# Expert results put to their tokens by TensorE job by job instead of through memory, a third short expert job, and the last weight unit in two transfers

## The reference, cut to what matters

```python
def _moe(xn, router, w_gu, w_down):
    logits = (xn @ router).astype(jnp.float32)
    top_v, top_i = lax.top_k(logits, TOP_K)          # 2 of 8 experts
    w = jax.nn.softmax(top_v, axis=-1)
    gates = jnp.sum(w[..., None] * jax.nn.one_hot(top_i, N_EXPERTS, dtype=jnp.float32), axis=-2)
    y = jnp.zeros_like(xn)
    for e in range(N_EXPERTS):
        y = y + gates[..., e:e + 1].astype(xn.dtype) * _swiglu(xn, w_gu[e], w_down[e])
    return y
...
x = x + _moe(_rmsnorm(x, norm_g[l, 1]), ...)
return _rmsnorm(x, final_norm_g)
```

## Time and profile before

| | before |
|---|---|
| median of 3 runs | 1277.41 us (1275.36 to 1279.4) |
| the profiled execution: device time | 1277.48 us |
| the profiled execution: span | 1275.7 us |
| TensorE busy | 1243.6 us (97%) |
| VectorE, ScalarE busy | 398.6 us (31%), 270.5 us (21%) |
| mean granted TensorE clock | 0.997 |
| bytes moved | 437.87 MB, mean 343 GB/s |

### The profile page before, as it was taken

How to read it: one execution, slowest core, us unless ns; L and a number is a source line. 1 busy time by engine, 2 the same in 40 slices (tenths; PEclk the granted TensorE clock), 3 DMA queues, 4 the chain that set the end, 5 groups by cost and what they waited for, 6 DMA issues and landing times.

```text
span 1275.7 us, 24518 instructions
## 1 busy us (share of the span) xinstructions
PE 1243.6 (97%) x11007; PEld 645.1 (51%) x11007; DVE 398.6 (31%) x665; ACT 270.5 (21%) x396; POOL 31.0 (2%) x71
## 2 busy tenths in 40 slices
PE   8999999999999999999989999999999999999975
PEld 7988888888888633333423333333333333333321
DVE  6886665677675502002002100300200030020022
ACT  6765455455464200000000000000000000000001
POOL 2000000002000100000000000000000000000010
PEclk9999999999999999999999999999999999999999
DMA  9654655556916899999999999999999999999995
GB/s 347 201 184 153 211 180 181 197 187 212 321 57 255 341 415 376 422 427 431 429 429 428 430 429 428 430 428 424 428 390 419 411 367 427 401 427 410 428 429 240
DMA packets 84836, 437.87 MB, mean 343 GB/s; under 512 B 4728, under 2 KB 47840, under 8 KB 61184
## 3 DMA queue, kind: packets, MB, share of 16 engines
q1 hardware_dynamic: 80896, 423.64, 82.3%
q0 software_dynamic: 2912, 10.06, 2.5%
q10 hardware_dynamic: 928, 2.68, 0.5%
HBM read 425.87 MB, written 10.49 MB: 342 GB/s over the span
## 4 chain that ended last, share of the span: by engine, by line
PE 91%; DMA 7%; DVE 1%; ACT 1%; issue 0%; ACTq 0%; DVEq 0%; POOLq 0%; SPq 0%; POOL 0%
PE bank L1915 40%; PE bank L1937 12%; PE bank L1565 8%; PE bank L1531 6%; PE bank L1944 6%; PE bank L1532 5%; PE bank L1533 5%; DMA ring<-in_moe_w_gu 4%; PE bank L1564 3%; DMA ring<-in_moe_w_down 3%; PE bank L1972 1%; PE bank L1645 1%; PE bank L1568 0%; PE bank L1822 0%; PE bank L1796 0%; PE bank L1768 0%
## 5 line engine op out<-in xcount | busy, mean ns | idle before, releaser
L1915 PE MATMUL bank<-ring,tokT 128*32 128x512 f32 (+1 forms) x5632 | 533.1, 539 | 2.5 <-DMA ring<-in_moe_w_gu 1.5
L1915 PEld LDWEIGHTS bank<-ring,tokT 128*32 128x32 f32 x5632 | 184.7, 110 | 348.0 <-issue 336.1
L1937 PE MATMUL bank<-ring,hT 128*32 128x512 f32 x1568 | 176.9, 592 | 3.9 <-DMA ring<-in_moe_w_down 3.9
L879 DVE TENSOR_TENSOR w_lo<-raw,w_hi 128x2048 fp32r<-128x2048 f32 x62 | 141.8, 2290 | 50.4 <-ACT w_hi L515 50.1
L1565 PE MATMUL bank<-act_parts,w_hi 128*128 128x512 f32 x368 | 127.5, 396 | 0.0
L1396 DVE TENSOR_TENSOR y_sb<-bank,yc_part 32x512 f32<-32x512 f32 x12 | 8.2, 684 | 377.4 <-ACT yc_part L810 377.3
L515 ACT ACTIVATE w_hi<-raw 128x2048 fp32r<-128x2048 f32 x62 | 118.4, 1913 | 28.1 <-PE bank L1533 28.1
L793 ACT ACTIVATE silu_e<-bank 128x1024 f32<-128x1024 f32 x8 | 8.2, 1024 | 493.4 <-PE bank L1915 493.4
L1937 PEld LDWEIGHTS bank<-ring,hT 128*32 128x32 f32 x1568 | 51.2, 110 | 120.3 <-issue 112.7
L1564 PE MATMUL bank<-act_parts,w_lo 128*128 128x256 f32 x322 | 89.8, 279 | 0.0
L1944 PE MATMUL bank<-ring,hT 128*32 128x512 f32 x672 | 79.8, 592 | 0.0
(11 more groups left out here) (331 smaller groups left out, 1080.3 us busy)
## 6 DMA issues: line engine op xcount, KB each, us to landing
ring<-in_moe_w_gu SPq DMA_DIRECT2D x128, 1792.0 KB, 15.2
ring<-in_moe_w_down SPq DMA_DIRECT2D x56, 2048.0 KB, 17.3
raw<-in_mlp_w_gu SPq DMA_DIRECT2D x22, 1024.0 KB, 4.9
raw<-in_mlp_w_down SPq DMA_DIRECT2D x11, 1024.0 KB, 4.8
raw<-in_lru_w_in SPq DMA_DIRECT2D x8, 1024.0 KB, 11.0
raw<-in_w_kvf SPq DMA_DIRECT2D x8, 1024.0 KB, 5.1
raw<-in_fox_w_qg SPq DMA_DIRECT2D x8, 1024.0 KB, 5.3
y_rows<-zeros POOLq DMA_DIRECT2D x17, 384.0 KB, 12.4
```

Source lines behind the costliest of these rows:

```text
L879: v.tensor_tensor(split_of(u)[1][:, :], raw[:, u % RAW, :], split_of(u)[0][:, :].bitcast(f32), ALU.subtract).then_inc(lo_done, 1)
L1915: last = t_.matmul(b[32 * t:32 * t + 32, 0:N1 if s else N0], tokT[:, g, k, :], of_tile[:, t, 4:7, :] if s else of_tile[:, t, 0:4, :], star ...
L1937: last = t_.matmul(y_ab_ps[32 * t:32 * t + 32, :], hidden_of(u, r, t % 2), w[:, lo:lo + HALF], start=u == 0 and r == 0, stop=u == 6 and r ...
```

## The change

Results of jobs 0 to 6 no longer go through `y_rows`. A table `place` is built once: for each of a token's two choices it holds, on every partition, the token's row number and its weight (`place_by_column`: eight diagonal matrices by VectorE, two matmuls with ones, one copy). For each job VectorE compares the row numbers with the slot numbers `slot_n` of the job and gets `w_T`, the weight of each token in each slot (`weights_by_slot`). TensorE multiplies `w_T` with `y_sb` (`place_y`, once for each 128 tokens, two matmuls of 128 x 512 each), into banks 6 and 7, and VectorE adds them to `x` (`add_y`). Third, `BY_COUNT` and `SHORT_OF` make job `middle + 3` (the fifth, job 4 where there are 8 jobs) short too. Last, the last down unit comes in two transfers of 1024 KB with a wait for each (`last_unit`), and the load of the final gain waits for the first matmuls of that unit.

```diff
-BY_COUNT = (0, 1, 3, 4, 5, 6, 7, 2)
+BY_COUNT = (0, 1, 4, 5, 3, 6, 7, 2)
...
-            for u in range(7):
+            for u in range(6):
                 sp.wait_ge(unit_used, used_in(last, u - 6))
                 down(last, last_expert, u)
+            sp.wait_ge(unit_used, used_in(last, 0))
+            for rr in range(2):
+                of = slice(2 * D * rr, 2 * D * rr + 2 * D)
+                sp.dma_start(deep_slot(6)[:, of], e_dn[last_expert][:, 6, of]).then_inc(slot_full[6 + rr], 16)
...
-            for j in range(NE - 1, ROUNDS * NE):
-                pool.dma_start(y_rows[CAP * j:CAP * j + CAP, :], zeros[0:CAP, :]).then_inc(y_blank, 16)
...
             pool.wait_ge(xsg_ready, NT)
+            pool.wait_ge(y_half, 1)
             pool.dma_start(gain_bc[:], final_norm_g.partition_broadcast(P)).then_inc(gfin_loaded, 16)
...
-            for t in range(NT):
-                for c, into in enumerate((xs, xs_g)):
-                    g.indirect_dma_start(out=into[:, t, :], out_offset=None, in_=y_rows[:, :],
-                                         in_offset=bass.IndirectOffsetOnAxis(ap=row_i[:, c, t:t + 1], axis=0)).then_inc(y_back[t][c], 16)
...
-                act.dma_start(y_rows[bass.ds(CAP * j, n), :], y_sb[0:n, :]).then_inc(y_stored, 16)
...
-                v.tensor_scalar(of_count(SHORT_OF), of_count(PLACE), float(2), None, ALU.is_le)
+                v.tensor_scalar(of_count(SHORT_OF), of_count(PLACE), float(3), None, ALU.is_le)
...
+            def add_y(j):
+                for t in range(NT):
+                    dve.wait_ge(y_placed, 2 * j + t + 1)
+                    v.tensor_tensor(x[:, t, :], banks2[3][:], x[:, t, :], ALU.add).then_inc(y_added, 1)
...
+                for n, of_token in enumerate((row_f[:, 0, :, :], gate_t[:])):
+                    for c in range(2):
+                        for t in range(NT):
+                            last = v.tensor_scalar(of_rows(n)[:, c, t, :], ident[:], of_token[:, c, t:t + 1], None, ALU.mult)
+                last.then_inc(diag_built, 1)
+                dve.wait_ge(place_done, 1)
+                v.tensor_copy(place[:].rearrange("p n c m -> p (n c m)"), banks2[3][:]).then_inc(place_ready, 1)
...
+                for c in range(2):
+                    last = v.scalar_tensor_tensor(out=w_T[0:CAP, c, :], in0=place[0:CAP, 0, c, :], scalar=slot_n[0:CAP, 0:1], in1=place[0:CAP, 1, c, :],
+                                                  op0=ALU.is_equal, op1=ALU.mult)
...
-            for n in range(4):
-                t, c = n // 2, n % 2
-                dve.wait_ge(y_back[t][c], 16)
-                v.scalar_tensor_tensor(out=x[:, t, :], in0=(xs, xs_g)[c][:, t, :], scalar=gate_t[:, c, t:t + 1], in1=x[:, t, :],
-                                       op0=ALU.mult, op1=ALU.add).then_inc(moe_added, 1)
...
+            def place_y(j, t, short=False):
+
+                n = SHORT if short else CAP
+                for half in range(2):
+                    last = t_.matmul(bank[6 + half], w_T[0:n, 0, t * P:(t + 1) * P], y_sb[0:n, HALF * half:HALF * half + HALF],
+                                     start=True, stop=True)
+                last.then_inc(y_placed, 1)
...
                 for k in range(KD):
-                    if more and k == 4:
+                    if k == 1:
                         pe.wait_ge(y_free_a, j + 1)
-                        pe.wait_ge(y_free_d, sums_now)
+                        pe.wait_ge(y_free_d, sums)
+                        pe.wait_ge(w_built, 2 * j + 2)
+                        place_y(j, 0, short)
+                    if k == 3:
+                        pe.wait_ge(y_added, 2 * j + 1)
+                        place_y(j, 1, short)
+                    if more and k == 5:
+                        pe.wait_ge(y_added, 2 * j + 2)
                         gather_tokens(j + 2)
```

More of the change, by code:

```diff
@@ L801, in expert_silu, with copy_y @@
                     a.activation(silu_e[:, C0:WIDTH], c_ps, ACT.Silu).then_inc(e_silu, 1)
-            def copy_y(j, stored=None, short=False):
+            def copy_y(j, short=False):
                 act.wait_ge(unit_used, used_in(j, 15))
-                if stored is not None:
-                    act.wait_ge(y_stored, stored)
                 for half in range(2):
@@ L1946, in down, with last_rounds @@
                 last.then_inc(unit_used, 1)
+            def last_rounds(w, u, half, rr):
+                for t in range(4):
+                    r = 2 * rr + t // 2
+                    lo = r * D + half * HALF
+                    last = t_.matmul(y_half_ps[half][32 * t:32 * t + 32, :], hidden_of(u, r, t % 2), w[:, lo:lo + HALF],
+                                     start=u == 0 and rr == 0, stop=u == 6 and rr == 1)
+                return last
             def last_down(fill, u):
@@ L1954, in last_down, with last_unit @@
                     for rr in range(2):
-                        for t in range(4):
-                            r = 2 * rr + t // 2
-                            lo = r * D + half * HALF
-                            last = t_.matmul(y_half_ps[half][32 * t:32 * t + 32, :], hidden_of(u, r, t % 2), w[:, lo:lo + HALF],
-                                             start=u == 0 and rr == 0, stop=u == 6 and rr == 1)
-                    if half == 1:
-                        last.then_inc(unit_used, 1)
-                    elif u == 6:
-                        last.then_inc(y_half, 1)
+                        last = last_rounds(w, u, half, rr)
+                last.then_inc(unit_used, 1)
+            def last_unit(j):
+                for rr in range(2):
+                    pe.wait_ge(slot_full[6 + rr], 32 * j + 48 if rr else 48 * j + 48)
+                    for half in range(2):
+                        last_rounds(deep_slot(6), 6, half, rr).then_inc(y_half, 1)
             def gather_tokens(j):
@@ L1974, in gather_tokens, with step @@
                 last.then_inc(tok_gathered, 1)
-            def step(j, sums, sums_now, short=False, next_short=False, more=True):
+            def place_y(j, t, short=False):
+                n = SHORT if short else CAP
+                for half in range(2):
+                    last = t_.matmul(bank[6 + half], w_T[0:n, 0, t * P:(t + 1) * P], y_sb[0:n, HALF * half:HALF * half + HALF],
+                                     start=True, stop=True)
+                last.then_inc(y_placed, 1)
+            def step(j, sums, short=False, next_short=False, more=True):
                 for k in range(KD):
@@ L1995, in last_job @@
             def last_job(j):
-                pe.wait_ge(y_free_a, j)
-                pe.wait_ge(y_free_d, j - 1)
+                pe.wait_ge(y_added, 2 * j)
                 pe.wait_ge(e_hT, j + 1)
-                for u in range(7):
+                for u in range(6):
                     if u == 2:
@@ L2020, in _ @@
             for k in range(KD):
+                if k == 1:
+                    pe.wait_ge(diag_built, 1)
+                    for n in range(2):
+                        last = t_.matmul(bank[6 + n], ones[:, 0:P], xs[:, 0, n * HALF:n * HALF + HALF], start=True, stop=True)
+                    last.then_inc(place_done, 1)
                 if k == 4:
+                    pe.wait_ge(place_ready, 1)
                     gather_tokens(1)
```

111 lines of the change are left out of this document (52 added, 59 removed).

## The result

| | before | after |
|---|---|---|
| median | 1278.05 us (4 runs) | 1262.34 us (1260.65 to 1263.26, 4 runs) |
| ratio, 95% interval | | 0.9878 [0.9857, 0.9899] |
| the profiled execution | 1277.48 us | 1260.65 us |
| its span | 1275.7 us | 1258.7 us |
| bytes moved | 437.87 MB | 426.29 MB |

The account below looks back on a forecast made before the run. TensorE's work and the weight stream bound the layer closely, TensorE deciding: 1277.5 - 36.1 (short job) - 12.0 - 1.0 (waits, slow starts) + 29.1 (placement) + 2.1 (table) + 1.1 + 0.9 (moved waits) = 1261.6 us; range 1254 to 1267.

Parts of the forecast that it names:

- Two limits close together, the later decides: Expert layer: sums along TensorE (1261.6 us) and the weight stream (1255.3) lie close; the later, TensorE's, sets the time.
- Third short job, -36.1: Job 4's gate, up and down units get shorter, taking 36.1 us off TensorE.
- Placement, 14 x 2.08 = 29.1: Placement matmuls, two halves for each of 7 jobs: 1.73 us plus 0.35 for tile width changes each, 29.1 us more.
- free: Rival, chance 0.17: changes of tile width at the placements cost nothing, so the time is about 1256 us.
- full drains: Rival, chance 0.08: each of 30 changes of tile width costs a record's length, so 1274.1 us.
- plain float32 with 512 columns is slower: Rival, chance 0.04: placement and table matmuls cost twice the price for a column, 26 us more, 1287.6 us.
- The table, 2.1 us: Building the table takes one more pair of matmuls on TensorE, 2.1 us, and delays the stream's start by that.
- The moved waits, 1.1 and 0.9: TensorE waits 1.1 us for hidden values behind job 4, and 0.9 in all for copied results before placements.
- Waits for weights, -12.0, and slow starts, -1.0: TensorE's 12.0 us of waits for weights in the layer go, and 1.0 us of slow starts in the last job's down units.
- the stores were free: Rival, chance 0.10: old stores and gathers took no share of the stream, which then bounds at 1264.5 us.
- Last unit in two transfers and the late gain, nothing: At the kernel's end, splitting the last unit's transfer and loading the gain late change nothing on TensorE's path.
- The stream's own sum, 1255.3: Along the weight stream: last landing at 1240.8 us, TensorE ending half a unit later at 1242.6, time 1255.3 us.

Follow-up runs that it names:

- 3: The changed kernel without its placement matmuls and VectorE's adds to x, results of jobs 0 to 6 missing from the output: 1257.1 us, ratio 0.9837.
- 9: The changed kernel without placement matmuls and adds to x, run once more as a mark on another chip: 1257.7 us, ratio 0.9839.
- 11: The changed kernel with placements in 32-wide tiles, job 6's second placement behind the last up unit, and a fourth short job: 1256.85 us, ratio 0.9839.
- 1: The changed kernel with the third short job undone, so only two short jobs: 1294.7 us, ratio 1.013.
- 2: The kernel before with the third short job alone, results still through memory: 1267.9 us, ratio 0.9918.
- 4: The changed kernel with each placement in tiles 32 wide, four side by side: 1259.2 us, ratio 0.9857.
- 7: The changed kernel with the two matmuls of each placement one unit apart: 1264.3 us, ratio 0.9896.
- 10: The changed kernel without placement matmuls and adds to x, but with each job's results stored to memory, unread: 1261.7 us, ratio 0.9885.
- 6: The changed kernel with the last unit in one transfer and the final gain loaded among the weights: 1261.65 us, ratio 0.9871.

## Why the prediction was right, point by point

- *Two limits close together, the later decides.* Right, and shown from both sides: with TensorE lightened (3, 9, 11) the time stops at 1257 to 1258 whatever is taken off; with TensorE loaded (1) it follows TensorE's sum within 1 us. The changed kernel stands 4 to 5 us above that limit, where I had 6.
- *Third short job, -36.1.* Right: undoing it costs 32.4 us where 36.1 - 2.8 = 33.3 was expected. Alone (2) it is worth 9.4 us only, because the stream takes the rest.
- *Placement, 14 x 2.08 = 29.1.* 14 x 2.05 = 28.7 by the chain. The price of the change of width, which I took from 64-wide tiles in the attention at 0.35 a pair, is 0.33 with 32-wide tiles (4 and 7). The agreement is a little lucky: I took 0.24 for two ordinary starts, where the earlier trace rows has 0.11 for one, so that row gives 0.37. The rivals "free" and "full drains" are both out, and so is "plain float32 with 512 columns is slower", as a placement's matmuls take 1.72 us without a change of width and 1.91 with it. The Trainium skill ("TensorEngine Tiling (Array Packing)", Key Properties) states that a change of the tiling mode drains TensorE; the traces agree in kind, at 0.33 us for a pair.
- *The table, 2.1 us.* Right. The timeline has its matmuls from 468.69 to 470.60, so 1.9 and what follows. It delays the stream as forecast: from the issue of job 0's first up unit to that of its first down unit were 76.2 us before (434.87 to 511.12) and are 78.3 after (432.74 to 511.05).
- *The moved waits, 1.1 and 0.9.* The second wait for hidden values cost 0.9 more, the placements waited 0.8 + 0.3. I had also named a wait for `y_sb` as a sign of being wrong; it came, but at the size that the sum had for it. The second placement never waited for VectorE's add, which took 1.22 us and not 1.5.
- *Waits for weights, -12.0, and slow starts, -1.0.* 1.7 us were left, so 10.3. Of five ends of 0.2 us one is left, so 5 x 3.64 - 17.38 = 0.8.
- By rows the layer's sum is then -36.1 - 10.3 - 0.8 + 28.7 + 2.0 + 0.9 + 1.1 = -14.5 us, against 14.9 measured in the layer and 15.9 forecast. The missing 1.4 is the 1.7 us of waits that were left, with small differences of the other terms on both sides.
- *Stores take stream time.* Right (10); "the stores were free" is out. With the stores and gathers kept, the stream decides: experiment 2 stands at 1267.9, 5.6 us above the changed kernel. The gathers were not tested by themselves.
- *Last unit in two transfers and the late gain, nothing.* Right within what (6) can tell. The gain was issued at 1245.92, landed 3.8 us later, and was needed at 1253.56.
- *The stream's own sum, 1255.3*, was about 2 us too low (1257.1 and 1257.7 measured). The 374 instead of 392 GB/s from 440 to 520 us isn't the reason: of the 3.4 us that it costs, 1.2 are the 512 KB of gain that left this stretch, and 2.2 are the table's delay, for which I had 2.1. What the sum lacked is the end of the stream. The last landing was at 1242.4 in experiment 3 and 1242.9 in 9, not at 1240.8, although the last transfer was issued at 1212.3 and 1212.8; and TensorE ended 2.3 us behind it, not 1.8. About 10 us before the last landing the flow falls to half, and then stays there, as it did in experiment 2 and not before. First the kernel before, then experiments 3 and 2:

```profile
1256.00:1258.00 2.00, 1.64 (x16) 0.55 (x20) 0.00 (x0) 0.00 (x0) 0.00 (x0) 1.00 1.01 434
...
1234.00:1236.00 2.00, 2.00 (x24) 0.65 (x20) 0.00 (x0) 0.00 (x0) 0.00 (x0) 1.00 0.49 209
...
1244.00:1248.00 4.00, 2.78 (x30) 0.68 (x24) 0.00 (x0) 0.00 (x0) 0.00 (x0) 1.00 0.53 225
```

The last landings of the kernel before and of experiment 2 are at 1261.2 and 1252.2. Over the last 12 us before the last landing, 2 us worth of full flow is missing in the kernel before, 6.5 in experiment 3 and 7 in experiment 2. That is 4 to 5 us more than before, and the misses were 2 and 3.1, so the parts don't add up to the us. Why the stream ends slowly is open.

## What to carry to other kernels

Where a weight stream and TensorE are within a per cent of each other, make both sums before changing either: what is taken off the one that isn't last becomes waits, and the same edit can be worth 32 us or 9 depending on what else is on the path. A trade can be right even if it loads the busier engine, as here, where 29 us of matmuls bought back the stream time of the stores and gathers, and this only because another edit had first freed 36 us. Among matmuls in narrow tiles, small extra products are best written in the same tile width: the columns cost the same, and the 0.33 us for a change of width and back go.

## What the runs showed of the hardware

Behind the 4.5 us that TensorE stands before the last job, the granted clock falls to its lower level (1.2 GHz) for a stretch, and how long differs from one execution to the next of the same kernel. The changed kernel's two profiled executions, in the same window:

```profile
1202.00:1245.00 43.00, 38.45 (x338) 11.80 (x338) 7.26 (x7) 0.00 (x0) 0.00 (x0) 0.92 0.93 396
```

is the second one; the first, shown above, has 0.96. That is 43 x 0.04 x 2 = 3.4 us at half speed in one and 6.9 in the other (the view gives 0.50 for 1226 to 1228 us of the second), and the first two down units took 8.69 us in the first and 9.81 in the second:

```profile
1223.83 9.81 PE L1957 MATMUL bank<-ring,hT 128*32 128x512 f32 x64 [4.55 <-DVE hT L1360]
```

So 1.1 us of the 3.4 us between these two executions (1260.65 and 1264.06) is this one stretch. Another 1.4 us has arisen by 14 us, where the same four matmuls (L1606) take 1.05 us in the first and 1.95 in the second, and 0.9 us is the longer waits for weights (1.7 and 2.6). Differences of 1 to 2 us between single profiles of this kernel are of that kind and say nothing on an edit.
